# Column sums by one-column matmuls in seven norms, values as stationary operand in two attentions, and a collection of expert outputs with ScalarE's help

## The reference

```python
def rms_norm(x, g):                       # eps 1e-6
    return x * rsqrt(mean(x * x, -1) + EPS) * g

def causal_block_attention(q, k, v, scale):        # MLA: 8 heads, q and k 96 wide, v 64 wide
    s = where(kpos <= qpos, q @ k.T * scale, -inf)
    return softmax(s) @ v

def first_block(x, ...):
    h = rms_norm(x, norm_attn)                                       # first norm
    q_mla, ckv, k_rope, qkv_dil, gate_pre = split(h @ w_in)
    o_mla = mla_branch(...)                                          # ends in causal_block_attention
    o_dil = dilated_branch(...)                                      # three groups, not changed
    x = x + (gates[0] * (o_mla @ w_o_mla) + gates[1] * (o_dil @ w_o_dil)) @ w_out
    h2 = rms_norm(x, norm_ffn)                                       # router norm
    return x + hier_moe(h2, ...)          # 32 experts, each token to two: y = w1 * e1(h2) + w2 * e2(h2)

def second_block(x, ...):                 # two layers
    for layer in range(2):
        h = rmsnorm(x, norm_mix_g[layer]) * (1 + scale_m) + shift_m  # block norm, then a split norm
        mixed = attention_head_groups(...) if layer == 0 else gated_deltanet(...)
        x = x + gate_m * mixed
        h = rmsnorm(x, norm_ffn_g[layer]) * (1 + scale_f) + shift_f  # two split norms
        x = x + gate_f * swiglu(h, ...)
    return rmsnorm(x, final_norm_g)                                  # final norm
```

## Time and profile before

| | |
|---|---|
| median of 3 runs | 2783.06 us (2780.72 to 2783.65) |
| profiled execution | 2791.62 us, span 2790.3 us |
| mean granted PE clock | 0.937 of full speed |
| busy: PE, PEld, DVE, ACT, POOL | 2534.1, 1996.1, 1327.3, 877.7, 446.4 us |
| share of PE in the chain that ended last | 75% |
| MLA attention | 472.8 to 529.6 us |
| collection and block norm | 1066.4 to 1119.2 us |
| MoBA attention | 1256.8 to 1310.4 us |

### The profile page before, as it was taken

The page is one execution under the profiler, slowest core; times in us unless marked ns, Lnnn a source line. Parts: engine busy times, 40 slices in busy tenths (PEclk is TensorE's granted clock), DMA queues, the critical chain, the costliest instruction groups (busy, mean ns, idle before and its releaser), DMA issues.

```text
span 2790.3 us, 32962 instructions
## 1 busy us (share of the span) xinstructions
PE 2534.1 (91%) x12977; PEld 1996.1 (72%) x12977; DVE 1327.3 (48%) x2244; ACT 877.7 (31%) x1568; POOL 446.4 (16%) x463
## 2 busy tenths in 40 slices
PE   6899989999699994997789999988989899899997
PEld 4799987767555552786468888856977877688886
DVE  7786754523411114416446675354745744433333
ACT  3354444422211111325533222234223322322222
POOL 4654503000123321300010000000300300100001
PEclk9899988999799996999889999988999999999998
DMA  5443412133379994320026575231012002232322
GB/s 191 136 128 112 146 32 77 31 91 98 152 300 406 403 400 151 97 84 1 1 76 189 177 222 152 76 84 38 1 35 57 1 23 76 80 95 86 110 81 70
DMA packets 315081, 332.38 MB, mean 119 GB/s; under 512 B 20848, under 2 KB 273904, under 8 KB 302512
## 3 DMA queue, kind: packets, MB, share of 16 engines
q1 hardware_dynamic: 292720, 281.73, 30.9%
q0 software_dynamic: 22208, 48.55, 5.1%
HBM read 372.15 MB, written 16.78 MB: 139 GB/s over the span
## 4 chain that ended last, share of the span: by engine, by line
PE 75%; DVE 6%; ACT 3%; DMA 1%; issue 1%; ACTq 0%; POOL 0%; DVEq 0%; POOLq 0%
PE bank L492 13%; PE bank L494 13%; PE bank L493 13%; PE bank L2212 6%; PE bank L3058 5%; PE bank L2238 3%; PE bank L1603 2%; PE bank L714 1%; PE bank L402 1%; PE bank L404 1%; PE bank L403 1%; PE bank L734 1%; PE bank L2197 1%; PE bank L2602 1%; PE bank L724 1%
## 5 line engine op out<-in xcount | busy, mean ns | idle before, releaser
L347 DVE TENSOR_TENSOR sb_w_lo<-sb_weights,sb_w_hi 128x1024 fp32r<-128x1024 f32 (+2 forms) x221 | 247.2, 1127 | 459.8 <-ACT sb_w_hi L341 459.5
L492 PE MATMUL bank<-sb_h_hi,sb_w_hi 128*128 128x512 f32 x1040 | 420.9, 405 | 7.1 <-DVE sb_w_lo L347 7.1
L494 PE MATMUL bank<-sb_h_hi,sb_w_lo 128*128 128x512 f32 x1040 | 408.4, 393 | 0.0
L493 PE MATMUL bank<-sb_h_lo,sb_w_hi 128*128 128x512 f32 x1040 | 408.3, 393 | 0.0
L341 ACT CAST sb_w_hi<-sb_weights 128x1024 fp32r<-128x1024 f32 x224 | 216.0, 972 | 511.6 <-PE bank L494 440.1
L492 PEld LDWEIGHTS bank<-sb_h_hi,sb_w_hi 128*128 128x128 f32 x1040 | 197.1, 190 | 62.4 <-issue 22.3
L493 PEld LDWEIGHTS bank<-sb_h_lo,sb_w_hi 128*128 128x128 f32 x1040 | 197.2, 190 | 45.4 <-issue 5.3
L494 PEld LDWEIGHTS bank<-sb_h_hi,sb_w_lo 128*128 128x128 f32 x1040 | 196.8, 189 | 42.4
L537 POOL TENSOR_TENSOR sb_scratch<-sb_scratch 128x512 f32<-128x512 f32 x30 | 38.6, 1288 | 1158.0 <-ACT sb_scratch L527 1158.0
L402 PE MATMUL bank<-sb_wide,sb_h_hi 128*128 128x512 f32 (+2 forms) x448 | 178.6, 399 | 9.9 <-DVE sb_wide L384 5.7
L404 PE MATMUL bank<-sb_wide,sb_h_lo 128*128 128x512 f32 (+2 forms) x448 | 172.1, 384 | 0.0
(11 more groups left out here) (541 smaller groups left out, 4722.2 us busy)
## 6 DMA issues: line engine op xcount, KB each, us to landing
sb_weights<-ffn_w_in SPq DMA_DIRECT2D x88, 512.0 KB
sb_weights<-w_in SPq DMA_DIRECT2D x52, 512.0 KB
sb_xT<-ada_w POOLq DMA_DIRECT2D x24, 1024.0 KB, 6.7
sb_weights<-ada_w SPq DMA_DIRECT2D x24, 1024.0 KB
sb_expert_weights<-w_down SPq DMA_DIRECT2D x22, 1024.0 KB
sb_expert_weights<-w_gate SPq DMA_DIRECT2D x20, 1024.0 KB
sb_expert_weights<-w_up SPq DMA_DIRECT2D x19, 1024.0 KB
sb_weights<-ffn_w_out SPq DMA_DIRECT2D x32, 512.0 KB
```

What stands on the lines that cost most here:

```text
L347: dve.tensor_tensor(u.lo[:, 0:u.kt, :], u.chunk.w, u.hi[:, 0:u.kt, :].bitcast(F32), ALU.subtract).then_inc(*k.lo.one())
L492: pe.matmul(bank[:], u.hi[:, kk, :], act[0][:, kk, :], start=first and kk == 0, stop=False)
L493: pe.matmul(bank[:], u.hi[:, kk, :], act[1][:, kk, :], start=False, stop=False)
L494: mm = pe.matmul(bank[:], u.lo[:, kk, :], act[0][:, kk, :], start=False, stop=last and kk == u.kt - 1)
```

## The change

**Norms.** The sum of squares is one moving column of ones against each 128x128 piece of the squares: one column per tile of tokens, so that root and reciprocal work on 128x4 (`k.roots`). `norm_spread_pe` then spreads the inverse over 128 partitions in bank 7, by four 128x128 matmuls with the column broadcast as stationary operand and the identity moving, and the rows read the inverse there. The table load is issued before the last square. In `split_norm` units 2 and 3 come after the shift rows.

**Attentions.** The MLA and MoBA attentions get their own functions `heads_attention_*`. A mask of 128x512 in `scr[10]` is made by POOL, and one DVE operation adds it, scales and takes the maximum. The values are stationary (64 columns), the turned probabilities move (128 columns), and two heads fill the two halves of the array's columns; weighing is done for two jobs at every odd step. The result is already turned; the inverted denominators are spread by eight matmuls into bank 7, copied by ACT, and DVE multiplies.

**Collection.** ACT scales the second rows and DVE's additions of a tile come after the multiply-add of the next; PE turns into alternate pairs of banks and sums the squares by one-column matmuls. The weight slots are freed only once tile 1 is gathered (`(k.collected[1], 32)`), so SP's loads of `attn_w_in` start then.

```diff
 first_norm:
-        pe.matmul(k.bank[3][:], k.const("ones"), k.scr[kk % 4][:], start=kk == 0, stop=kk == KD - 1
-                  ).then_inc(*k.summed.one())
+        for i in range(NT):
+            mm = pe.matmul(k.bank[3][:, i:i + 1], k.scr[kk % 4][:, i * P:(i + 1) * P], k.const("ones")[:, 0:1],
+                           start=kk == 0 and i == 0, stop=kk == KD - 1, skip_group_check=True)
+        mm.then_inc(*k.summed.one())
...
 fold_act:
+    if j == KD - 1:
+        root_table_act(k)
...
+def norm_spread_pe(k):
+    pe = k.nc.tensor
+    pe.wait_ge(*k.h_inv.at(1))
+    for i in range(NT):
+        mm = pe.matmul(k.bank[7][:, i * P:(i + 1) * P], k.roots[:, i:i + 1].to_broadcast([P, P]), k.const("ident"),
+                       start=True, stop=True)
+    mm.then_inc(*k.h_wide.one())
...
 split_norm:
     norm_sum_pe(k)
-    root_table_act(k)
-    split_hi_act(k, units[0])
     norm_root_act(k, k.h_sum.at(1))
-    for u in units[1:4]:
+    for u in units[0:2]:
         split_hi_act(k, u)
     split_lo_pool(k, units[1])
     norm_shift_act(k, shift, split)
+    for u in units[2:4]:
+        split_hi_act(k, u)
+    norm_inverse_dve(k)
+    norm_spread_pe(k)
     split_lo_dve(k, units[0])
-    norm_rows_dve(k, gain, shift, split, units[2])
+    norm_rows_dve(k, gain, shift, split)
+    split_lo_dve(k, units[2])
     split_lo_dve(k, units[3])
...
 block_norm:
-    norm_sum_pe(k)
-    root_table_act(k)
+    norm_root_act(k, None)
     block_hi_act(k, blocks[0])
-    block_lo_dve(k, blocks[0])
-    norm_root_act(k, k.h_sum.at(1))
...
+def heads_attention_pe(k, jobs):
...
+        t = s - 4
+        if 0 <= t < len(jobs) and t % 2 == 1:
+            i, a = jobs[t].tile, jobs[t].h // 2
+            bank = k.bank[5 + i % 2]
+            pe.wait_ge(*k.dve_copied.at(t // 2 + 1))
+            pe.wait_ge(*k.act_copied.at(t // 2 + 1))
...
+            for b in range(i + 1):
+                for odd in range(2):
+                    mm = pe.matmul(bank[odd * HD:(odd + 1) * HD, a * P:(a + 1) * P], jobs[t - 1 + odd].values[b],
+                                   k.scr[4 + (t - 1 + odd) % 4][:, b * P:(b + 1) * P], start=b == 0, stop=b == i)
+            mm.then_inc(*k.weighed.one())
...
+            for h in range(H):
+                mm = pe.matmul(k.bank[7][h % 2 * HD:(h % 2 + 1) * HD, h // 2 * P:(h // 2 + 1) * P],
+                               k.den[:, i, h:h + 1].to_broadcast([P, HD]), k.const("ident"), start=True, stop=True)
+            mm.then_inc(*k.finished.one())
...
 collect_pe:
-            if i >= 1:
-                pe.wait_ge(*k.added.at(2 * (i - 1) + half + 1))
+            if i >= 2:
+                pe.wait_ge(*k.added.at(2 * (i - 2) + half + 1))
...
-        slot.freed, slot.held = list(k.recent.values()), slot
+        slot.freed, slot.held = list(k.recent.values()) + [(k.collected[1], 32)], slot
```

More of the change, by code:

```diff
@@ L570, in norm_shift_act, with norm_inverse_dve, norm_rows_dve @@
                            ).then_inc(*k.h_hi.one())
-def norm_rows_dve(k, gain, shift, split, late=None):
+def norm_inverse_dve(k):
+    k.nc.vector.wait_ge(*k.h_root.at(1))
+    k.nc.vector.reciprocal(k.roots[:], k.roots[:]).then_inc(*k.h_inv.one())
+def norm_rows_dve(k, gain, shift, split):
     dve = k.nc.vector
[L575 to L578, removed]
+    inv = k.bank[7]
+    dve.wait_ge(*k.h_wide.at(1))
     for kk in range(KD + 1):
@@ new lines, in heads_attention_act @@
+def heads_attention_act(k, jobs):
+    act = k.nc.scalar
+    for s in range(len(jobs) + 7):
+        if s < len(jobs):
+            j = jobs[s]
+            act.wait_ge(*k.maxed.at(s + 1))
+            if s >= 4:
+                act.wait_ge(*k.turned.at(s - 3))
+            act.activation(k.scr[s % 4][:, 0:j.n], k.bank[s % 3][:, 0:j.n], ACT.Exp, bias=j.negmax, scale=-1.0,
+                           accum_out=j.den).then_inc(*k.exped.one())
+        t = s - 2
+        if 0 <= t < len(jobs) and t % 2 == 1:
+            act.wait_ge(*k.turned.at(t + 1))
+            if t >= 4:
+                act.wait_ge(*k.weighed.at(t // 2 - 1))
+            act.copy(k.scr[4 + t % 4][:, 0:jobs[t].n], k.bank[3 + t % 2][:, 0:jobs[t].n]
+                     ).then_inc(*k.act_copied.one())
+        t = s - 5
+        if 0 <= t < len(jobs) and jobs[t].h == H - 1:
+            i = jobs[t].tile
+            act.wait_ge(*k.finished.at(i + 1))
+            if i >= 2:
+                act.wait_ge(*k.evacuated.at(i - 1))
+            act.copy(k.scr[8 + i % 2][:], k.bank[7][:]).then_inc(*k.mixed_in.one())
@@ L736, in attention_pe, with attention_act @@
             mm.then_inc(*k.weighed.one())
[L737 to L740, removed]
-            if i >= 1:
[L742 to L749, removed]
+def attention_act(k, jobs, blocks):
     act = k.nc.scalar
@@ L769, in attention_act, with attention_dve @@
                      ).then_inc(*k.act_copied.one())
[L770 to L778, removed]
+def attention_dve(k, jobs, out):
     dve = k.nc.vector
@@ new lines, in collect_bank, with collect_act @@
+def collect_bank(k, i, half):
+    return k.bank[4 * (i % 2) + half]
+def collect_act(k, r, pairs):
+    act = k.nc.scalar
+    root_table_act(k)
+    for i in range(NT + 1):
+        if i < NT:
+            b = pairs[i % 3][1]
+            act.wait_ge(k.collected[i], 32)
+            act.activation(b, b, ACT.Identity, scale=r.stat[:, 5, i:i + 1]).then_inc(*k.gained.one())
+        for n in range(2 * (i - 1), 2 * i) if i else ():
+            act.wait_ge(*k.added.at(n + 1))
+            if n >= 2:
+                act.wait_ge(*k.summed.at(n - 1))
+            act.activation(k.scr[11 + n % 2][:].rearrange("p (a t) -> p a t", a=4),
+                           k.xT[:, 4 * (n % 2):4 * (n % 2) + 4, (i - 1) * P:i * P], ACT.Square
+                           ).then_inc(*k.squared.one())
@@ L2332, in collect_sum_dve, with collect_sums_pe @@
+def collect_sums_pe(k, i):
+    pe = k.nc.tensor
     for half in range(2):
         n = 2 * i + half
[L2334 to L2339 removed]
@@ L2342, in collect_act @@
-def collect_act(k):
-    act = k.nc.scalar
-    for n in range(2 * NT):
-        i, half = n // 2, n % 2
-        act.wait_ge(*k.added.at(n + 1))
-        if n >= 2:
-            act.wait_ge(*k.reduced.at(n - 1))
-        act.activation(k.scr[11 + n % 2][:].rearrange("p (a t) -> p a t", a=4),
-                       k.xT[:, 4 * half:4 * half + 4, i * P:(i + 1) * P], ACT.Square).then_inc(*k.squared.one())
+        pe.wait_ge(*k.squared.at(n + 1))
+        for a in range(4):
+            mm = pe.matmul(k.bank[3][:, i:i + 1], k.scr[11 + n % 2][:, a * P:(a + 1) * P], k.const("ones")[:, 0:1],
+                           start=n == 0 and a == 0, stop=half == 1 and a == 3, skip_group_check=True)
```

186 lines of the change are left out of this document (114 added, 72 removed).

## The result

The changed kernel's median is 2771.74 us (2761.53 to 2777.09, 8 runs) against 2783.36 (2780.72 to 2789.43, 8 runs): ratio 0.9948, 95% interval [0.9935, 0.9961], 11.6 us less. Forecast were 2741 and 42 us. The direction was right, the size and the range (2725 to 2761) were wrong. The runs of the changed kernel spread over 16 us, and go with the mean granted clock (0.946 in the fastest, 0.940 in the slowest).

The account below looks back on a forecast made before the run. TensorE (PE) was taken as three quarters of the bounding chain. Attentions -6.2 and -8.1, norms -17.6 and collection -10.4 summed to -42.3 us, from the median 2783.06 to 2741, range 2725 to 2761.

Parts of the forecast that it names:

- Attentions: MLA and MoBA attentions: two-head weighing saves 0.095 a block at full clock; MLA -6.2 us, MoBA -8.1.
- The slow start of the MLA attention: MLA attention, tiles 0 and 1 at the 1.2 GHz level: 24 blocks save 0.08 each, within MLA's -6.2 us.
- The 1.5 us where DVE leads in MoBA: MoBA attention from 1265, DVE busy 4.66 of 5.00: one DVE operation for three, worth -1.5 us.
- A sum in the bounds: Both attentions, bound: with no block cheaper they end 0.8 us above before.
- Rival B: Two-head weighing in the attentions: loads not hidden, 0.22 us a block, no saving there; 2761 us, chance 0.10.
- Collection: End of the experts: earlier gathers and a shorter chain, last tile's sums 0.8 to 1.6; gain 10.4 us, bounds -13 to -6.
- The write's 3.4: Collection: holding four weight loads lets the last write of y land sooner, first gathers 3.4 us earlier.
- Split norms: Three split norms: shorter root and reciprocal, table load moved out; -2.9, -3.0 and -2.9 us.
- final and router: Final and router norms: short root and reciprocal, router's table load moved ahead; -2.3 and -2.1 us.
- First norm: First norm: 64 one-column records, 12.8 us against 10.06, offset by a shorter reciprocal; taken as 0, bounds +3 and -2.
- Rival F: Rows of four norms slowed by POOL's lo of unit 1, 1.4 to 2.5 us each; 2749 us, chance 0.08.
- Rival C: Clock rises sooner, in the MLA attention or at one norm's restart: 5 us less, 2736 us, chance 0.12.

Follow-up runs that it names:

- weights_early: Changed kernel with the four attn_w_in loads released at the barrier again; from the write to the root 38.8 us for 36.8.
- split_old: Changed kernel with the three split norms put back as before; 2774.17 us, ratio to before 0.9966.
- Pair 1: First profile of the changed kernel compared stage by stage with the first of before; stage shifts sum to -19.8 us.
- quad: Changed kernel weighing four jobs at every fourth step, with six buffers in place of four; 2768.20 us, ratio to before 0.9922.

## Why the forecast was wrong, step by step

- **Attentions, the step that failed** (14.3 us forecast for both, some 3 in the medians). Block 0.118 (0.115) and spread 0.97 (0.92) were right. Not in the sum: 16 odd steps in each attention pass from 128 to 64 columns and back. An added passage costs 0.30 us. Against the kernel before it is less, since a score matmul behind a weighing took 0.91 there too, for 0.86 behind transposes: two steps at tile 3 went from 4.38 to 3.82 (1283.29 above to 1287.11 here), 0.56 less where the forecast had 0.76. So an odd step lost 0.2 of its gain, some 6 us for both attentions at full clock. Nor was the stall behind L835 at a tile's end in the sum, 0.6 us at tile 1's (1.2 at tile 0's in the MLA attention, next to none at tile 2's). To the end: 5.2 forecast, ten odd steps 2.0, stall 0.6, dearer blocks and spreads 0.3, leaves 2.3: measured 2.2.

```profile
1286.08 1.09 PE L768 MATMUL bank<-sb_scratch,sb_arena 128*64 128x128 f32 x16
1287.11 1.12 PE L748 MATMUL bank<-sb_arena 128*128 128x512 f32 x2
```

- **The slow start of the MLA attention.** From the first exponential to its end it took 53.9 us before and 53.1 after, 0.8 less for 6.2. Its second tile ran 13.3 us in place of 11.6: the 1.2 of stall, and a spread that fell almost wholly at the 1.2 GHz level and took 1.67 for 0.92.
- **The 1.5 us where DVE leads in MoBA** did not show: the first two tiles there took 16.4 to 18.5 us in the profiles with the new attentions as they stand, 16.5 to 17.7 in the three of before.
- **A sum in the bounds.** With no block cheaper the attentions end 0.5 above before by the terms given (-14.3 + 14.8), not 0.8; nothing hangs on it.
- **Rival B and the rule behind it.** The rule that loads overlap only where row groups differ (the Trainium skill, "TensorE: Matmul & The Clock Gate", Part 3, The mechanism) would have put 0.22 on a block. The weighing's 0.118 disagrees with it inside a run of one width. At each passage 0.1 us and more appears on both sides, and there a load may well stand bare; the runs show the price, not its cause.
- **Collection, a term mis-sized.** I priced a tile's sums at 0.8 to 1.6, that is 8 records; eight matmuls leave 16, 3.4 us at the low clock, and two tiles' worth stand at the end. Measured 6.83 for 0.8 to 1.6. The root came 5.4 late: 3.7 behind tile 3's scaling, and 1.8 in tile 3's gather, which was issued 0.8 later than forecast (T0 + 7.4) and landed slower. `weights_early` gives 1.4 of that 1.8 to the held weights, inside the bound that I gave. The write's 3.4 was right.
- **Norms.** Split norms right in sum (8.8; 9.3 by `split_old`), final and router within 0.9 us. First norm: 2 us dearer, inside its bounds; I had the 12.8 us for its 64 records on paper and still took 0, and the gain of up to 2 beside POOL did not come either.
- **Rival F** (rows slowed by POOL): did not happen; rows with one input in PSUM took 0.70 each beside POOL.
- **Clock.** Rival C spoke of a gain only. Pair 1 lost 7 us in a stage that the change doesn't touch, 5.3 of it in the last part, which moves by 4.8 between profiles of before too; I had no case for the low-clock share moving up there. And I worked from one profile that lay 8.6 above the median; the second profile of before (2783.7) lies at the median, 12.0 above the changed kernel's first.

The range of the terms (2732 to 2750) took their bounds half at a time. The one term with no bound, the passage, was in no row of before that I had asked for, though the stick-breaking attention passes too. That the time fell at all is no proof of the attentions' mechanism: with the attentions of before (`att_old`) the ratio was 0.9955 still, so the norms and the collection carried it.

## What to carry to other kernels

When work moves to another width of PE's array, price the passages, not only the matmuls: 0.30 us there and back here. Fewer and longer runs of such work save passages, but alone they made this attention longer (`quad`), because the other engines' order then waited at the runs' ends and more work was left for the tail. Count the records of a small matmul from a row of the same kind (two for each here), at the clock that PE will have there. A stretch that ends in the middle of a pipeline can leave work out; measure to a point where both kernels have done the same. A sum of small gains spread over a program whose clock moves by a few us a stage needs more than one profile of before.

## What the runs showed of the hardware

- A pass between 128-column and 64-column matmuls and back costs PE 0.30 us at full clock, by added transposes (1.51 us for five, 3.32 for eleven).
- A 128x1 matmul on 32-bit data costs 0.43 us at the 1.2 GHz level (16 of them 6.83 us in the collection, at a granted clock of 0.50); 32 of them took 13.8 us in the first norm.
- DVE beside a running POOL subtraction: a 128x512 operation with both inputs in SBUF took 2.81 us and ended half a us after POOL's, where one with an input in PSUM took 0.7.
- In the delta net up to 2250 the granted clock cost the same within 0.15 us in three profiles of the kernel before; in its last part two of the same three took 4.8 us less. With the earlier stages changed it cost other amounts, and not always the same for one kernel (4.4 and 1.4 us).
